# Router by token tile in plain fp32, and a gather that reads its rows with a stride

## The reference

```
scores = sigmoid(xt @ router_w)                       # 256 tokens x 16 experts
sel = scores + router_b
group_score = sum of the two best sel in each of 4 groups;  best group wins
idx = the two best experts inside the best group
gates = scores[idx] / sum(scores[idx]), placed at idx, zero elsewhere
for e in range(16):                                   # each expert is 1024 -> 256 -> 1024
    out += gates[:, e] * ((silu(xt @ w_gate[e]) * (xt @ w_up[e])) @ w_down[e])
```

## Time and profile before

| | |
|---|---|
| three runs | 828.68, 832.18, 832.49 us; median 832.18 us |
| the profiled execution: its own time | 830.09 us |
| its span, first to last instruction | 828.4 us |
| mean granted clock of TensorE | 0.971 |
| busy: PE / PEld / DVE / ACT / POOL | 751.5 / 608.4 / 404.2 / 279.7 / 46.3 us |
| read from HBM | 174.18 MB |

### The profile page before, as it was taken

How to read it: one execution, slowest core, us unless ns; L and a number is a source line. 1 busy time by engine, 2 the same in 40 slices (tenths; PEclk the granted TensorE clock), 3 DMA queues, 4 the chain that set the end, 5 groups by cost and what they waited for, 6 DMA issues and landing times.

```text
span 828.4 us, 12485 instructions
## 1 busy us (share of the span) xinstructions
PE 751.5 (91%) x5028; PEld 608.4 (73%) x5028; DVE 404.2 (49%) x703; ACT 279.7 (34%) x480; POOL 46.3 (6%) x88
## 2 busy tenths in 40 slices
PE   4998899999898989999789988999998989899983
PEld 4987787779788866555489877787797889655641
DVE  4774965664538412121357568647535383121115
ACT  4455343445524121111134454335435141211111
POOL 3400000000005000000010000001000010000000
PEclk9999999999999999999889999999999999999997
DMA  9981224584338259999944320356642450799991
GB/s 280 349 268 51 78 76 150 190 269 152 104 124 312 66 211 396 420 416 415 354 158 125 130 98 31 100 180 204 207 156 95 162 194 21 305 398 416 417 373 54
DMA packets 62529, 176.14 MB, mean 213 GB/s; under 512 B 3856, under 2 KB 37056, under 8 KB 53248
## 3 DMA queue, kind: packets, MB, share of 16 engines
q1 hardware_dynamic: 57856, 162.80, 53.8%
q0 software_dynamic: 4032, 12.24, 4.8%
q10 hardware_dynamic: 576, 0.20, 0.1%
HBM read 174.18 MB, written 1.05 MB: 212 GB/s over the span
## 4 chain that ended last, share of the span: by engine, by line
PE 67%; DVE 15%; DMA 5%; issue 4%; DVEq 4%; ACT 3%; POOL 0%; ACTq 0%; POOLq 0%; SPq 0%
PE ring L1784 12%; PE ring L1817 6%; PE quad L1418 5%; PE ring L1418 5%; PE quad L1419 5%; PE quad L1420 5%; PE ring L1420 5%; PE ring L1419 5%; DMA w_raw<-in_moe_w_down 4%; PE quad L1829 3%; DVE w_lo L868 3%; PE ring L1691 2%; PE ring L1670 2%; PE quad L1734 1%; PE quad L1735 1%
## 5 line engine op out<-in xcount | busy, mean ns | idle before, releaser
L868 DVE TENSOR_TENSOR w_lo<-raw,w_hi 128x1024 fp32r<-128x1024 f32 (+1 forms) x116 | 133.4, 1191 | 93.1 <-ACT w_hi L604 90.3
L1418 PE MATMUL ring<-x_hi,w_hi 128*128 128x256 f32 x480 | 143.2, 298 | 16.0 <-DVE x_lo L887 5.5
L1419 PE MATMUL ring<-x_lo,w_hi 128*128 128x256 f32 x480 | 140.4, 292 | 0.0
L1420 PE MATMUL ring<-x_hi,w_lo 128*128 128x256 f32 x480 | 140.3, 292 | 0.0
L604 ACT CAST w_hi<-raw 128x1024 fp32r<-128x1024 f32 (+1 forms) x116 | 112.5, 1021 | 81.8 <-PE quad L1420 73.5
L1418 PEld LDWEIGHTS ring<-x_hi,w_hi 128*128 128x128 f32 x480 | 97.0, 202 | 20.8 <-issue 10.9
L1419 PEld LDWEIGHTS ring<-x_lo,w_hi 128*128 128x128 f32 x480 | 96.9, 202 | 0.5 <-issue 0.5
L1420 PEld LDWEIGHTS ring<-x_hi,w_lo 128*128 128x128 f32 x480 | 96.8, 202 | 0.0
L1784 PE MATMUL ring<-raw,x_slots 128*64 128x256 f32 x512 | 61.5, 397 | 7.6 <-ACT arena L816 4.4
L622 ACT ACTIVATE arena<-ring 128x512 f32<-128x512 f32 (+1 forms) x68 | 36.5, 569 | 80.7 <-PE ring L1420 68.5
L1784 PEld LDWEIGHTS ring<-raw,x_slots 128*64 128x64 f32 x512 | 39.2, 143 | 29.9 <-issue 11.0
(11 more groups left out here) (282 smaller groups left out, 1244.9 us busy)
## 6 DMA issues: line engine op xcount, KB each, us to landing
raw<-in_moe_w_gate SPq DMA_DIRECT2D x24, 1024.0 KB, 8.1
raw<-in_moe_w_up SPq DMA_DIRECT2D x20, 1024.0 KB, 9.4
w_raw<-in_moe_w_down SPq DMA_DIRECT2D x16, 1024.0 KB, 12.4
raw<-in_moe_w_down SPq DMA_DIRECT2D x16, 1024.0 KB, 11.0
raw<-in_w_in SPq DMA_DIRECT2D x14, 1024.0 KB, 11.5
w_raw<-in_moe_w_up SPq DMA_DIRECT2D x12, 1024.0 KB, 7.9
raw<-in_xattn_wk SPq DMA_DIRECT2D x8, 1024.0 KB, 6.6
raw<-in_w_out SPq DMA_DIRECT2D x8, 1024.0 KB, 4.9
```

The costliest lines, as they stand in the source:

```text
L868: last = nc.vector.tensor_tensor(unit_slot(u, 1, n)[:, s], raw[:, SLOT[u], s], unit_slot(u, 0, n)[:, s].bitcast(F32), ALU.subtract)
L1418: mm(out, a_hi, b_hi, start=first, stop=False)
L1419: mm(out, a_hi, b_lo, start=False, stop=False)
L1420: return mm(out, a_lo, b_hi, start=False, stop=last)
```

## The change

- `X`'s turned tiles are copied as they are to one fp32 tile `xT` (which lies where `x_hi` lay): ACT copies banks xc0, xc1 and xc2, DVE copies xc3. The four `x_lo` instructions of this place are gone.
- The logits are made per token tile: `logits(t)` has 8 plain fp32 matmuls with `xT` stationary (128x128) and the router's weights `rw` moving (16 columns). They come out with tokens on the rows, so the copy to `logitsT` and the turns back are gone, and ACT takes the exponential per tile.
- `xn_hi` and `xn_lo` are written in natural order, reading `X` without a step. The step of 8 elements moves to the stationary operand of the gather (`rows_of`).
- `rw` is loaded once as fp32; its split at the start (L688 on ACT, L1032 and L1033 on DVE) is gone. The dense branch uses `xT` as well.
- The number of dummy matmuls is set anew in places.

```diff
-    jobs += [(f"xc{i}", "dve") for i in range(4)]
-    jobs += [("rt0", "act"), ("rt1", "act")]
+    jobs += [("xc0", "act"), ("xc1", "act"), ("rt0", "act"), ("xc2", "act"), ("xc3", "dve"), ("rt1", "act")]
...
+        xT = x_slots[:, 0, :, :]
...
-        xn_hi = rounded("xn_hi", 0, T, DC, P)
-        xn_lo = rounded("xn_lo", 2048, T, DC, P)
+        xn_hi = rounded("xn_hi", 0, T, D)
+        xn_lo = rounded("xn_lo", 2048, T, D)
...
-                x_high("xc", l)
-                for t in range(T):
-                    nc.scalar.copy(xn_hi[:, t], X[:, t, :].rearrange("p (q c) -> p c q", c=DC)).then_inc(xn_hi_done, 1)
-                move("rt0", l, logitsT, bank("rt0")[:, 0:SEQ])
-                act.wait_ge(misc_ready, misc_done("rt1", l))
-                nc.scalar.activation(rt[:, 1], bank("rt1")[:, 0:SEQ].rearrange("p (t e) -> p t e", t=T)[:, :, 0:E],
-                                     ACT.Exp, scale=-1.0).then_inc(act_emptied, 1)
+                turned_x(0)
+                turned_x(1)
+                nc.scalar.copy(xn_hi[:, 0, :], X[:, 0, :]).then_inc(xn_hi_done, 1)
+                logits_exp(0)
+                turned_x(2)
+                nc.scalar.copy(xn_hi[:, 1, :], X[:, 1, :]).then_inc(xn_hi_done, 1)
+                logits_exp(1)
...
-                x_low("xc", l, 3)
+                dve.wait_ge(misc_ready, misc_done("xc3", l))
+                nc.vector.tensor_copy(xT[:, 4:8, P:2 * P], bank("xc3").rearrange("p (a b) -> p a b", a=4)).then_inc(dve_emptied, 1)
...
+                def logits(t):
+
+                    o = free(f"rt{t}", l)
+                    for k in range(DC):
+                        r = mm(o[:, 0:E], xT[:, k, t * P:(t + 1) * P], rw[:, k, :], start=k == 0, stop=k == DC - 1)
+                    r.then_inc(misc_ready, 1)
+
+                keep_busy("xc2", l, 19)
+                transpose_x("xc", l, 2, (0,))
+                keep_busy("xc2", l, 4)
...
+                logits(0)
+                transpose_x("xc", l, 2, (1,))
+                keep_busy("rt1", l, 3)
+                pe.wait_ge(act_emptied, emptied("xc2", l))
                 pe.wait_ge(dve_emptied, emptied("xc3", l))
...
+                logits(1)
 
-                keep_busy("gb0", l, 26)
+                keep_busy("gb1", l, 26)
...
+                def rows_of(x_part, t, c):
+                    return x_part[:, t, :].rearrange("p (q c) -> p c q", c=DC)[:, c, :]
...
-                                mm(o, xn_hi[:, t, 2 * r + c, :], sl, start=t == 0, stop=False)
-                                last = mm(o, xn_lo[:, t, 2 * r + c, :], sl, start=False, stop=t == T - 1)
+                                mm(o, rows_of(xn_hi, t, 2 * r + c), sl, start=t == 0, stop=False)
+                                last = mm(o, rows_of(xn_lo, t, 2 * r + c), sl, start=False, stop=t == T - 1)
```

More of the change, by code:

```diff
@@ L203, in hybrid_trunk_kernel @@
         pinv = sb("pinv", [P, 2, PAD + 1])
-        rw = sb("rw", [P, 3 * P], F32R)
-        rw_hi, rw_lo = (rw[:, i * P:(i + 1) * P].rearrange("p (c e) -> p c e", c=DC) for i in range(2))
+        rw = sb("rw", [P, DC, E])
         rb = sb("rb", [P, E])
@@ L405, in hybrid_trunk_kernel @@
         rope_sined = sem("rope_sined")
-        rwhi = sem("rwhi")
         stored = sem("stored")
@@ L656, in _ @@
                 act.dma_start(freq[:, 1:2], rope_sign.rearrange("(p a) -> p a", a=1)).then_inc(pre_full, 16)
-            act.dma_start(rwraw, router_w.rearrange("(p c) e -> p c e", c=DC)).then_inc(rw_full, 16)
+            act.dma_start(rw[:], router_w.rearrange("(p c) e -> p c e", c=DC)).then_inc(rw_full, 16)
             def norm_stats(n, l):
@@ L686, in _ @@
                     act.drain().then_inc(rope_sined, 1)
-                    act.wait_ge(rw_full, 16)
-                    nc.scalar.copy(rw_hi, rwraw).then_inc(rwhi, 1)
                 move("cq", l, cT[:, 0:2, :], bank2("cq"), unit=0)
@@ L784, in _, with turned_x, logits_exp @@
                 norm_stats(1, l)
-                x_high("xc", l)
-                for t in range(T):
-                    nc.scalar.copy(xn_hi[:, t], X[:, t, :].rearrange("p (q c) -> p c q", c=DC)).then_inc(xn_hi_done, 1)
-                move("rt0", l, logitsT, bank("rt0")[:, 0:SEQ])
-                act.wait_ge(misc_ready, misc_done("rt1", l))
-                nc.scalar.activation(rt[:, 1], bank("rt1")[:, 0:SEQ].rearrange("p (t e) -> p t e", t=T)[:, :, 0:E],
-                                     ACT.Exp, scale=-1.0).then_inc(act_emptied, 1)
+                def turned_x(j):
+                    t, c = j // 2, 4 * (j % 2)
+                    move(f"xc{j}", l, xT[:, c:c + 4, t * P:(t + 1) * P], bank(f"xc{j}").rearrange("p (a b) -> p a b", a=4))
+                def logits_exp(t):
+                    act.wait_ge(misc_ready, misc_done(f"rt{t}", l))
+                    nc.scalar.activation(rt[:, 1, t, :], bank(f"rt{t}")[:, 0:E], ACT.Exp, scale=-1.0).then_inc(act_emptied, 1)
+                turned_x(0)
[5 more added lines that the diff above has]
+                logits_exp(1)
                 def tanh(dst, src, e, n):
@@ L883, in x_low @@
                         halfway()
-                    dve.wait_ge(xhi_done, l * 16 + (4 * n + j + 1))
+                    dve.wait_ge(xhi_done, l * 12 + (4 * n + j + 1))
                     t, c = j // 2, 4 * (j % 2)
@@ L1236, in _ @@
                 layer_norm(1, l, unit_used, used(U_O + 3, l))
-                x_low("xc", l, 3)
+                dve.wait_ge(misc_ready, misc_done("xc3", l))
+                nc.vector.tensor_copy(xT[:, 4:8, P:2 * P], bank("xc3").rearrange("p (a b) -> p a b", a=4)).then_inc(dve_emptied, 1)
                 for t in range(T):
                     dve.wait_ge(xn_hi_done, l * T + t + 1)
-                    last = nc.vector.tensor_tensor(xn_lo[:, t], X[:, t, :].rearrange("p (q c) -> p c q", c=DC),
-                                                   xn_hi[:, t].bitcast(F32), ALU.subtract)
+                    last = nc.vector.tensor_tensor(xn_lo[:, t, :], X[:, t, :],
+                                                   xn_hi[:, t, :].bitcast(F32), ALU.subtract)
                 last.then_inc(xn_lo_done, 1)
@@ L1460, in keep_busy, with transpose_x @@
                     mm(o[:, 0:P], ident[:], ident[:], start=True, stop=True)
-            def transpose_x(name, l, n):
-                for j in range(4):
+            def transpose_x(name, l, n, tiles=range(T)):
+                for j in (2 * t + i for t in tiles for i in range(2)):
                     t, c0 = j // 2, 4 * (j % 2)
@@ L1470, in transpose_x @@
                     else:
-                        if n != 1 and j % 2 == 0:
-                            keep_busy(f"{name}3", l, ((19, 6) if n else (26, 12))[t])
+                        if n == 0 and j % 2 == 0:
+                            keep_busy(f"{name}3", l, (26, 12)[t])
                         pe.wait_ge(x_ready, l * (3 * T) + (n * T + t + 1))
@@ L1696, in _ @@
                     into_quad(y_hi, y_lo, 2 * i, 2, U_O + i, l, i == 0, i == 3)
-                transpose_x("xc", l, 2)
-                keep_busy("rt0", l, 4)
-                pe.wait_ge(dve_emptied, emptied("xc3", l))
[L1701 to L1710, removed]
-                keep_busy("gb0", l, 26)
+                def logits(t):
[6 more added lines that the diff above has]
+                keep_busy("xc2", l, 4)
+                if l == 0:
+                    pe.wait_ge(rw_full, 16)
+                pe.wait_ge(act_emptied, emptied("xc1", l))
+                logits(0)
+                transpose_x("xc", l, 2, (1,))
+                keep_busy("rt1", l, 3)
+                pe.wait_ge(act_emptied, emptied("xc2", l))
+                pe.wait_ge(dve_emptied, emptied("xc3", l))
+                logits(1)
+                keep_busy("gb1", l, 26)
                 pe.wait_ge(member_ready, l + 1)
@@ L1881, in moe_in @@
                             for k in range(DC):
-                                for i, x_part in enumerate((x_hi, x_lo)):
-                                    r = mm(ring[:, b, c * SEQ:(c + 1) * SEQ], w[:, k, c * P:(c + 1) * P],
-                                           x_part[:, k, :].bitcast(F32), start=k == 0 and i == 0, stop=k == DC - 1 and i == 1)
+                                r = mm(ring[:, b, c * SEQ:(c + 1) * SEQ], w[:, k, c * P:(c + 1) * P], xT[:, k, :],
+                                       start=k == 0, stop=k == DC - 1)
                         r.then_inc(unit_used, 1)
```

7 lines of the change are left out of this document (1 added, 6 removed).

## The result

The changed kernel took 853.23 us (median of four runs, 852.07 to 859.89), the kernel before 830.6 in its four: the ratio is 1.0267, with a 95% interval of 1.022 to 1.0314. It is slower by 2.7%. The forecast was 824.4 and faster. The profiled execution has a span of 851.6 us, 23.2 more than before. The ratios of this document leave out executions over 1.5% above the fastest of their kernel (one of e5's twelve, at 832.18 us, and one of the kernel before beside it, at 1903.6 us).

The account below looks back on a forecast made before the run. PE holds 67% of the chain, but in the routers DVE's rest of x ends last. Mean 830.9 less 6.5 (3.4 layer 0, 3.1 layer 1), with gather, stream and clock at 0, gave 824.4 us; range 820.5 to 830.5.

Parts of the forecast that it names:

- The step that failed: Gather's 128 matmuls a layer: strided stationary loads cost nothing extra, distance staying 0.12 us, judged by X's strided transposes.
- The rival that came true: Gather pays for the step, up to 0.10 us on each of 2 x 128 matmuls: 849 us, slower, chance 0.12.
- the page's rule: Sign for the gather rival: SBUF lines have 16 bytes, and reads touching another line each time pay a penalty.
- The router: Both routers, from tile 1's transposes to the counts: 9.76 us in each layer, gaining 3.4 and 3.1, together 6.5.
- 16 records: Router logits of one token tile on PE: 8 fp32 matmuls, two records each, 0.108 us a record, 1.73 in all.
- The rests: DVE's two instructions making the rest of x in the router: 1.23 us each, 2.45 together, instead of 4.20.
- The case in which the rests keep their 2.12 us: Router, DVE not sped up: each layer loses 1.8 us, 2.9 gain left, 828; within the main case of 0.76.
- the dummies: 26 dummies behind logits(1), 5.9 us, keep PE until 268.65; the counts could start at 268.6.
- The stream: Weight stream behind the gather: start and end move with PE, so the router's gain is kept.
- The clock: PE's granted clock around gate(0): a dip costs 1.7 us an occurrence; 0 was put in the sum.
- two dips to each side: Allowance for clock dips added or taken away: 3.4 us either way.
- The range: Whole kernel: 820.5 to 830.5 us, leaving out the strided gather and the tails, about 0.19.

Follow-up runs that it names:

- e5: Changed kernel with xn written so two chunks lie beside one another, the gather reading with a step of 2: 825.83 us, ratio 0.9941 to the kernel before.
- e1: Kernel before plus series of 16 dummy matmuls ahead of gather(0) with various steps; fp32r loads 0.112 us apart at step 1, 0.238 at step 8.
- e2: Kernel before with only natural-order xn and the strided gather, router as before: 867.32 us, ratio 1.0448.
- e7: Kernel before plus dummy series of strided transposes, stationary and moving operands, each behind contiguous matmuls; transposes 0.116 us apart at step 1, 0.118 at step 8.
- e3: Changed kernel with xn written in gather order, so the gather reads without a step: 828.1 us, ratio 0.9979 to the kernel before.
- e4: Changed kernel with expert features in natural order, no strided reads, gate and up weights in 1 KB pieces: 844.86 us, ratio 1.0148 to the kernel before.
- e6: Changed kernel with X, its transposes and the gather read at step 2, gate and up weights in 2 KB pieces: 832.99 us, ratio 1.0026 to the kernel before.
- e8: Like e5, but four chunks beside one another and the gather reading with a step of 4: 855.19 us, ratio 1.0311 to the kernel before.

## Why the prediction was wrong

*The step that failed* is the gather's: "I take none, since the transposes are the same engine and the same step". The strided load costs 0.24 us where 0.12 was taken, 256 times: by e1 256 x 0.12 = 31 us, by the chain 30.8. e2 has the loss without the rest of the change, e5 removes it by nothing but the order of the elements. The rows were right and the inference was not. A transpose is no measure for the load of a matmul: with a step it costs nothing (e7), while an fp32r or plain fp32 matmul pays by the line (e1). Why the transpose is spared is not shown. The rows had a possible sign that the two differ: a contiguous load had 140 ns in a transpose and 188 in the gather. The nearest row by engine and step was the wrong one; by the kind of access, ACT and DVE, which doubled, were nearer.

*The rival that came true* was priced at 849 and given 0.12. Its place and mechanism were right. Its price was 0.10 a matmul against 0.12 measured, and it left the clock out. By the page's rule, which the prediction named beside it (the Trainium skill, "Advanced Engine Details and Errata", section SBUF Cachelines), the trace agrees for fp32r and fp32 matmuls: another 16-byte line for each element costs, two elements a line nearly nothing. It does not agree for the fp32 transposes, which pay nothing at step 8 (e7), nor for the moving operand, which takes twice the time at step 2 already, with two elements in each line (e7).

*The router, step by step.* Right in its total, and in part by luck. logits(0) did not hold up tile 1 (transposes at 258.90, before 258.89). 16 records took 1.82 and 1.93 us on the chain against 1.73. The rests took 2.35 against 2.45, the scores started 3.99 behind the transposes against 4.5, and the counts came 9.63 and 9.62 behind them against 9.76. 6.75 us were gained there against 6.5. But the gain was put down to the wrong source. The case in which the rests keep their 2.12 us was priced at 2.9 left; e3 is that case and its routers kept 5.4. Two sizes were off. The prediction had the rests start 2.1 behind the transposes, and they start 1.62 behind. And the dummies bind by more than its "next to nothing": the score instruction that the counts wait for ended at 267.85, the dummies at 268.53, and this caps what shorter rests can give.

*The stream* moved with PE, as was said: the loads of 308.50 went out at 316.30, and it ran at 417 GB/s from 355 to 375 us, 414 before. e4 and e6 show the size of what it decides once it is slowed.

*The clock* was given 0 with two dips to each side. Counting the stretch from the gates to the end of gate(0), it cost 1.7 in the two layers before and 6.5 in the changed kernel, 4.8 more; in layer 0 the second dip of before, 1.7, was gone. The net of 3.1 lies within the 3.4 that was allowed. Six routers with a slow gather (changed kernel, e2, e8) took 8.7 to 12.0 us there, ten with a quick one (before, e3 to e6) 7.07 to 10.4, three of them at 7.07. That a slow gather lowers the clock is likely by this, and not shown: e3 reached 10.4 without it, e8 8.7 with it.

*The range* left out 836 to 849 as less than 2 in 10. The bound from ACT and DVE should have weighed more than 0.12, since the only row against it was of another operation.

## What to carry to other kernels

Where a step is moved from one engine to another, look at what each engine pays for it and how often: here, in each layer, four instructions were relieved of about 1 us each, of which the chain kept 0.7 in all, and 128 matmuls took 0.12 us more each, all of it on the chain. Before a strided operand goes to a matmul, count the 16-byte lines of its load: up to 64 were nearly free in these runs (0.118 us against 0.112), 128 doubled it. A middle layout (runs of two elements) can serve writer and reader at once, which neither the natural nor the turned order did.

## What was not expected of the hardware

- A stationary operand's load took 1.81 to 1.88 ns for each 16-byte line from 96 lines on (0.174 us at 96; 0.236 to 0.240 at 128), with 16, 128 or 256 moving columns alike in fp32r, and 0.237 at 128 lines in plain fp32.
- fp32 transposes with a 32-byte step: 0.118 us apart against 0.116 without one, at a granted clock of 1.00 (e7). At 0.50 they were 0.217 apart without a step (e1).
- A moving operand with step 2 and one with step 4: both 0.9 ns an element, against 0.43 without a step.
- In e1 the granted clock from 276.2 to 302 us, in which PE was busy all the time, mostly with strided loads, was 0.67, and 0.50 from 282.7 to 294 us. The distance of strided loads at step 8 was 0.238 there and 0.240 at 1.00 in e7.
- Between 355 and 375 us the weight stream, its queue full, ran at 414 GB/s where the gate and up weights came in pieces of 8 KB, at 392 with 2 KB and at 364 with 1 KB.
